# Low halves of streamed weights moved from GpSimd to VectorE in a single-core transformer kernel

## The reference

```
first_block:   h += 0.5 * swiglu(rmsnorm(h))                        # MLP1
               n  = rmsnorm(h);  z = n @ w_in                       # MIX1
               attn_o = sliding-window attention with rope and sinks(z)
               gla_o  = chunked gated linear attention(z), rmsnorm, * silu(gate)
               h += concat(attn_o, gla_o) @ w_out
               h += 0.5 * swiglu(rmsnorm(h))                        # MLP2
               h += sigmoid(rmsnorm(h) @ w_gate) * rmsnorm(p @ w_proj)   # PLE
second_block:  x += even_mixer(rmsnorm(x))      # EVEN: short conv and differential attention
               x += mem_attention(rmsnorm(x), rmsnorm(mem))         # CROSS0, 256 memory rows
               x += conv_ffn(rmsnorm(x))        # CONV0: up, conv of width 3, silu * value, down
               x += odd_mixer(rmsnorm(x))       # ODD: stick-breaking attention, 16 heads
               x += mem_attention(...)          # CROSS1
               x += conv_ffn(...)               # CONV1
```

## Time and profile before

| | |
|---|---|
| median of 3 runs | 2725.68 us |
| profiled execution | 2733.84 us |
| its span | 2731.7 us |
| busy: TensorE | 2626.6 us, 96% |
| busy: VectorE | 1462.8 us, 54% |
| busy: ScalarE | 908.0 us, 33% |
| busy: GpSimd | 473.1 us, 17% |
| mean granted TensorE clock | 0.985 |

### The profile page before, as it was taken

The page is one execution under the profiler, slowest core; times in us unless marked ns, Lnnn a source line. Parts: engine busy times, 40 slices in busy tenths (PEclk is TensorE's granted clock), DMA queues, the critical chain, the costliest instruction groups (busy, mean ns, idle before and its releaser), DMA issues.

```text
span 2731.7 us, 32426 instructions
## 1 busy us (share of the span) xinstructions
PE 2626.6 (96%) x12690; PEld 2147.6 (79%) x12690; DVE 1462.8 (54%) x1847; ACT 908.0 (33%) x1186; POOL 473.1 (17%) x352
## 2 busy tenths in 40 slices
PE   8999999889999988998999999999999999999999
PEld 6888877668888867876787888887886788888887
DVE  5444455665444467165543766565136554474745
ACT  4221243443211134433442423233136243332322
POOL 0000023122000013423453000003420354200000
PEclk9999999999999999999999999999999999999999
DMA  5222231013223222211332222323310133122222
GB/s 173 93 92 98 98 123 63 32 47 100 93 92 101 95 101 83 93 52 63 107 103 83 77 94 92 107 86 117 104 51 1 58 115 106 63 93 92 92 101 84
DMA packets 36597, 240.68 MB, mean 88 GB/s; under 512 B 3952, under 2 KB 6912, under 8 KB 8320
## 3 DMA queue, kind: packets, MB, share of 16 engines
q1 hardware_dynamic: 35008, 234.12, 24.9%
q10 hardware_dynamic: 1472, 4.94, 0.5%
HBM read 236.94 MB, written 2.10 MB: 88 GB/s over the span
## 4 chain that ended last, share of the span: by engine, by line
PE 87%; DVE 8%; ACT 2%; issue 1%; DMA 0%; DVEq 0%; SPq 0%; ACTq 0%
PE ps L494 23%; PE ps L495 23%; PE ps L496 23%; PE ps L1053 1%; PE ps L1006 1%; DVE op_lo L1602 1%; PE ps L978 1%; PE ps L512 1%; PE ps L511 1%; PE ps L510 1%; DVE sums L1616 1%; PE ps L522 1%; PE ps L606 1%; PE ps L607 1%; PE ps L608 1%
## 5 line engine op out<-in xcount | busy, mean ns | idle before, releaser
L494 PE MATMUL ps<-op_hi,w_hi 128*128 128x512 f32 x2160 | 856.7, 397 | 31.2 <-DVE op_lo L1602 21.3
L495 PE MATMUL ps<-op_lo,w_hi 128*128 128x512 f32 x2160 | 845.8, 392 | 0.0
L496 PE MATMUL ps<-op_hi,w_lo 128*128 128x512 f32 x2160 | 845.6, 392 | 0.0
L448 POOL TENSOR_TENSOR w_lo<-w_raw,w_hi 128x512 fp32r<-128x512 f32 x348 | 472.9, 1390 | 1892.5 <-ACT w_hi L1107 1892.3
L1107 ACT ACTIVATE w_hi<-w_raw 128x2048 fp32r<-128x2048 f32 x217 | 414.1, 1908 | 530.7 <-PE ps L496 404.8
L494 PEld LDWEIGHTS ps<-op_hi,w_hi 128*128 128x128 f32 x2160 | 408.9, 189 | 125.8 <-issue 20.1
L495 PEld LDWEIGHTS ps<-op_lo,w_hi 128*128 128x128 f32 x2160 | 408.9, 189 | 89.1 <-issue 4.9
L496 PEld LDWEIGHTS ps<-op_hi,w_lo 128*128 128x128 f32 x2160 | 408.6, 189 | 86.4
L1688 DVE TENSOR_TENSOR w_lo<-w_raw,w_hi 128x2048 fp32r<-128x2048 f32 x130 | 298.1, 2293 | 20.9 <-ACT w_hi L1107 8.1
L1653 DVE SCALAR_TENSOR_TENSOR x<-ps,x 128x512 f32<-128x512 f32 x134 | 92.6, 691 | 367.9 <-PE ps L496 357.4
L494 PE MATMUL ps<-h_hi,w_hi 128*128 128x512 f32 x692 | 273.4, 395 | 0.0
(11 more groups left out here) (286 smaller groups left out, 3070.2 us busy)
## 6 DMA issues: line engine op xcount, KB each, us to landing
w_raw<-in_wstream_dram SPq DMA_DIRECT2D x217, 1024.0 KB, 4.8
w_raw<-in_wstream_dram SPq DMA_DIRECT2D x8, 256.0 KB, 7.5
x<-in_x_dram SPq DMA_DIRECT2D x4, 512.0 KB, 7.1
cr_m<-in_mem_dram ACTq DMA_DIRECT2D x2, 1024.0 KB, 4.8
out_dram<-x SPq DMA_DIRECT2D x3, 512.0 KB, 2.6
ev_s<-in_alibi_dram ACTq DMA_DIRECT2D x1, 1024.0 KB, 4.8
m_c<-in_rope_dram ACTq DMA_DIRECT2D x1, 704.0 KB, 6.0
pl_p<-in_p_dram ACTq DMA_DIRECT2D x1, 512.0 KB, 3.6
```

Source lines behind the costliest of these rows:

```text
L448: ins = nc.gpsimd.tensor_tensor(w_lo[:, c % 4, at], w_raw[:, c % 2, at], w_hi[:, c % 4, at].bitcast(FP32), ALU.subtract)
L494: mm_(o, w_hi[:, c % 4, w], hi[:, k, 0:cols], start=(k == 0), stop=False)
L495: mm_(o, w_hi[:, c % 4, w], lo[:, k, 0:cols], start=False, stop=False)
L496: mm = mm_(o, w_lo[:, c % 4, w], hi[:, k, 0:cols], start=False, stop=(k == kt - 1))
```

## The change

GpSimd's program is removed. VectorE makes the low halves of all slabs with `low`, at hand-set points:

- `update_and_norm` calls `low(c + d + 3)` after each of the first three `onto_x` in every stage (in CROSS from the second on), not in MLPs alone.
- `mlp` begins with `low(at + 2)` where it waited for `w_ready`.
- In `attention` a `low` stands one iteration after each `between`.
- MIX1, EVEN and ODD have a `low` ahead of the first `use_rs_x` and after each `keep`; one of them stands right ahead of the sliding attention.
- In the gated linear attention `gl_scaled(l)` moves ahead of the `keep` at levels 3 and 6, and level 5 has a `low` behind it; another follows the output loop.
- PLE has a `low` before and after the last sums of squares and after each of three gates. CROSS has two ahead of the first `use_rs_x`, one ahead of its first `keep`, one after each `norm_queries`, one after `keep_values(0)`, and one an iteration after each of its entries in `CROSS_ENDS`.

```diff
-        @block.gpsimd
-        def _(pool):
-            def low(c):
-                n = SLAB // PIECES
-                for q in range(PIECES):
-                    at = slice(q * n, (q + 1) * n)
-                    ins = nc.gpsimd.tensor_tensor(w_lo[:, c % 4, at], w_raw[:, c % 2, at],
-                                                  w_hi[:, c % 4, at].bitcast(FP32), ALU.subtract)
-                ins.then_inc(w_ready, 1)
...
             def update_and_norm(...):
                 for d in range(DOWN - 1):
                     onto_x(c + d, d, 0, scale)
-                    if lows:
+                    if d >= first:
                         low(c + d + 3)
...
-                dve.wait_ge(w_ready, at + MLP_FIRST)
+                low(at + 2)
                 low(at + 3)
                 use_rs_x()
...
+                    if i - 1 in ends:
+                        low(c + ends[i - 1] + 3)
                     if i in ends:
                         between(ends[i])
...
             keep(c + 5, [m1_gk[:, 0, :], m1_gk[:, 1, :]])
+            low(c + 8)
             v.tensor_scalar(neg_sinks[:], gcol("sinks", 0, 8), -1.0, None, ALU.mult)
...
+                gl_scaled(l)
                 if l == 3:
                     keep(c + 8, [m1_gog[:, 0, :], m1_gog[:, 1, :]])
+                elif l == 5:
+                    low(c + 11)
                 elif l == 6:
                     keep(c + 9, [m1_gog[:, 2, :], m1_gog[:, 3, :]])
-                gl_scaled(l)
...
             keep_embedding(3, KT)
+            low(AT_PLE + 2)
             for k in range(KT):
                 add_squares(k)
+            low(AT_PLE + 3)
...
             for d in range(DOWN - 1):
                 gate(d)
+                low(AT_PLE + 4 + d)
...
+                low(at + 4)
                 for h in range(4):
                     keep(at + h, [cr_q[:, 2 * h, :], cr_q[:, 2 * h + 1, :]])
                     add_pair(h)
                     if h:
                         norm_queries(h - 1)
+                        low(at + h + 4)
...
             for d in range(4):
                 keep_rows(AT_ODD + 8 + d, od_v[:, :, d * 256:(d + 1) * 256])
+                low(AT_ODD + d + 11)
```

More of the change, by code:

```diff
@@ L56 @@
 PIECES = 4
-MLP_FIRST, MLP_END = 3, MLP_SLABS + 2
 TRI = 13 * P
@@ L1689, in low, with update_and_norm @@
                                 ALU.subtract).then_inc(w_ready, 1)
-            def update_and_norm(c, name, scale=1.0, also=None, early=False, lows=False):
+            def update_and_norm(c, name, scale=1.0, also=None, early=False, first=0):
                 for d in range(DOWN - 1):
                     onto_x(c + d, d, 0, scale)
-                    if lows:
+                    if d >= first:
                         low(c + d + 3)
@@ L1772, in mlp @@
                 n["taps"] += 2 * FT if conv else 0
-                update_and_norm(at + 24 + GROUPS[2], name, scale, also, early=True, lows=True)
+                update_and_norm(at + 24 + GROUPS[2], name, scale, also, early=True)
             def maxima(it, width, sinks=None):
@@ L1810, in probabilities, with attention @@
                     done(p_ready)
-            def attention(N, maxs, probs, outs, between, ends, beside={}):
+            def attention(N, maxs, probs, outs, c, between, ends, beside={}):
                 i0 = n["it"]
@@ L1850, in _ @@
             mlp(AT_MLP1, "mix")
+            c = AT_MIX1
+            low(c + 2)
             use_rs_x()
-            c = AT_MIX1
             cos, sin = m1_c[:, 0:SEQ], m1_c[:, SEQ:2 * SEQ]
@@ L1868, in _ @@
             keep(c, [m1_q[:, 0, :], m1_q[:, 1, :]])
+            low(c + 3)
             keep(c + 1, [m1_q[:, 2, :], m1_q[:, 3, :]])
+            low(c + 4)
             for t in range(2):
@@ L1872, in _ @@
             keep(c + 2, [m1_k[:], sums[0:16, :]])
+            low(c + 5)
             dve.wait_ge(aux["m1_c"], 16)
@@ L1885, in _ @@
                 rotated(m1_q[:, t, :])
+            low(c + 6)
             head_norm([m1_k[:]], [gcol("k")])
@@ L1888, in _ @@
             rotated(m1_k[:])
+            low(c + 7)
             dve.wait_ge(gate_ready, 1)
@@ L2021, in _ @@
                 operand(4 + h, tmp[:])
+            low(c + 12)
             update_and_norm(AT_MIX1 + MIX1_SLABS, "ffn2")
@@ L2071, in _ @@
                 gate(d)
+                low(AT_PLE + 4 + d)
             norm_x("mix0", lambda: gate(DOWN - 1))
+            low(AT_EVEN + 2)
             use_rs_x()
@@ L2120, in _ @@
                         head_norm([heads[t]], [gcol("eq" if t < 4 else "ek")])
+                low(c + d + 3)
             keep_rows(c + 5, ev_v[:, :, 256:512])
+            low(c + 8)
             dve.wait_ge(aux["lam"], 16)
@@ L2165, in cross @@
             def cross(at, layer):
+                low(at + 2)
+                low(at + 3)
                 use_rs_x()
@@ L2213, in cross @@
                 norm_queries(3)
+                low(at + 8)
                 norm_keys(0)
                 keep_values(0)
+                low(at + 9)
                 i0, N = n["it"], len(CROSS_ITEMS)
@@ L2245, in cross @@
                             keep_values(g)
+                    if i - 1 in CROSS_ENDS:
+                        low(at + CROSS_ENDS[i - 1] + 4)
                 n["it"] += N
-                update_and_norm(at + CROSS_SLABS, f"f{layer}")
+                update_and_norm(at + CROSS_SLABS, f"f{layer}", first=1)
             cross(AT_CROSS0, 0)
@@ L2251, in _ @@
             mlp(AT_CONV0, "mix1", True, 1.0)
+            low(AT_ODD + 2)
             use_rs_x()
@@ L2256, in _ @@
                 keep(AT_ODD + d, [od_q[:, 2 * d, :], od_q[:, 2 * d + 1, :]], scale=0.125)
+                low(AT_ODD + d + 3)
             for d in range(4):
                 keep(AT_ODD + 4 + d, [od_k[:, 2 * d, :], od_k[:, 2 * d + 1, :]])
+                low(AT_ODD + d + 7)
             for d in range(4):
                 keep_rows(AT_ODD + 8 + d, od_v[:, :, d * 256:(d + 1) * 256])
+                low(AT_ODD + d + 11)
             def softplus(t, kb):
```

4 lines of the change are left out of this document (2 added, 2 removed).

## The result

The kernel after takes 2699.65 us (median of 4 runs, 2698.73 to 2703.06), against 2726.43 us of the kernel before (median of 4 runs beside it, 2724.35 to 2728.99). The ratio is 0.9904, with a 95% interval of 0.9886 to 0.9921, which is small but clear of 1: faster by 26.8 us, where 26.6 us were forecast. The profiled execution after took 2699.93 us, its span is 2697.7 us.

The account below looks back on a forecast made before the run. TensorE was taken to bound the kernel, so time could change only where it stops or runs at a lower clock. Gains of -29.9 and costs of +3.3 make -26.6 us: 2699 us, range 2687 to 2717 us.

Parts of the forecast that it names:

- Rival 4: VectorE's stretched operations are not GpSimd's doing, so the added lows cost: slower, 2736 us; chance 0.04.
- The three starts: Entries to MIX1, ODD and PLE: stretched operations shorten, TensorE's stops and clock loss shrink or go: -4.9, -4.9, -8.7 us.
- rival 1: TensorE's stops shorten but the clock doesn't come back, with less from levels and PLE to EVEN: 2709 us; chance 0.22.
- Levels, -3.3: Gated linear attention: gl_scaled ahead of the keep shortens TensorE's stops of 3.03 and 1.61 us: -3.3 us.
- Sliding attention, +2.2: A low right ahead of the sliding attention's first maxima delays the probabilities TensorE waits for: +2.2 us, between 0 and 2.3.
- PLE's gates, -2.7: PLE to EVEN: relieved gate operations give about 9.5 us, three lows take 6.9, EVEN's op_lo comes earlier: -2.7 us.
- EVEN: Stretched probabilities ahead of a stop of 1.74 us, -1.4 us; stretched cast and subtraction at the output, -1.3 us.
- ODD's output: The same stretched cast and subtraction as at EVEN's output, with no low ahead: -1.8 us.
- rival 2: More gain: EVEN's entry and two output stops go wholly warm, PLE to EVEN gives -6: 2689 us; chance 0.11.
- CROSS1: A cost of +0.1 us in this stage, beside +0.5 us for the low ahead of CROSS's first keep.
- Rival 5: VectorE's lows block on w_hi, exposed in the attentions; sign: wait over 15 us; 2731 us at 14 exposed; chance 0.04.
- Rival 3: Stage starts: freed time turns into waits for ScalarE's op_hi; with costs at upper ends (+3.7), 2724 us; chance 0.07.

Follow-up runs that it names:

- changed_again: The kernel after the change, unaltered, run again as the base of a group of runs: 2698.44 us, ratio 0.9900 to the kernel before.
- pool_writes: The kernel after, with GpSimd given eight memsets per slab in MIX1, PLE and EVEN that read nothing and that nobody waits for: 2699.32 us, ratio 0.9897.
- pool_reads: The kernel after, with GpSimd given eight subtractions per slab in MIX1, PLE and EVEN that read SBUF and that nobody waits for: 2723.54 us, ratio 0.9985.
- pool_whole: The kernel before, with GpSimd's four pieces of each slab joined to one instruction of 128x2048: 2754.58 us, ratio 1.0100.
- entries_only: The kernel before, with only the third slab of MIX1, PLE and ODD moved from GpSimd to VectorE: 2711.08 us, ratio 0.9936.
- keep_ahead: The kernel after, with the two keep calls at levels 3 and 6 put ahead of gl_scaled again: 2699.41 us.
- three_later: The kernel after, with three lows (sliding attention, level 5, PLE's third gate) moved to where VectorE was idle: 2694.75 us and, measured again, 2696.67 us.

## Why the prediction was right

The sum was 26.6 us and the medians give 26.8; in two groups of the experiments the same TensorE and VectorE programs gained 28.3 us (changed_again) and 29.7 us (pool_writes). The mechanism is the forecast's. That the sum fits to 0.2 us is luck: terms that were off cancel, as the table shows.

- *Contention as the cause: shown.* Recreated without any dependency it takes 24 of 30 us back, if in part in other places than they were gained (pool_reads), and without GpSimd's reads nothing is lost (pool_writes). Rival 4 is out. The size that I took from the rows, 0.8 to 1.0 us an operation, was right for the pieces of 128x512; the reason behind it was incomplete. I set the rows against a full lock; pool_whole shows that there is one, and the ends of pieces and operations show that the rows are its result with alternating turns, 1.67 to 1.70 us for each pair of a piece and an operation. The four operations of rows 6 also add up to 6.56 us, not to 6.44.
- *The three starts.* -4.9, -4.9 and -8.7 forecast; 4.8, 4.7 and 9.7 in the profiles; entries_only, which does these alone, gave 18 of 18.5 us. PLE's stops came out at 3.67 and 0.55 us (3.6 and under 1 forecast; the second is 1.76 us in changed_again). The clock terms came with them: MIX1 begins at a granted clock of 1.00, so that rival 1 is out where stops went. The size of that term, 2.1 us, doesn't follow from its figures, though, which give 4.4 - 13 x 0.23 = 1.4; of the 4.8 us of the matched traces 3.0 are there when the stop ends, which leaves 1.7 for it.
- *Levels, -3.3: the term's reason failed.* I held that the wait of a `keep` ahead of `gl_scaled` fed TensorE's stops and that the reordering ends them. keep_ahead shows that it gives nothing: ScalarE's `gl_a` is as late. With the old order and without GpSimd it gained 3.6 us from the end of the sliding attention to behind the levels, the two profiles of the change 2.5 and 3.6. So what the levels gained is the missing contention (2.9 us by the earlier trace rows, of which I had given 2.3 to the low). The 1.5 us of the line "first levels" are the moved `keep` alone: keep_ahead has nothing there, and has caught up 7 us later. TensorE's waits for L741's kind sum to 7.8 us, as forecast (some 8), but 3.4 of them are ScalarE's now.
- *Sliding attention, +2.2: too large, by how much is open.* The low delays the start by 2.15 us, as the row said. The profiles with it lose 0.8 to 2.3 us in the stage, those with the low moved 0 to 1.4. The granted clock changes between executions within this stage, and by as much as the term.
- *PLE's gates, -2.7:* 1.8. The stretches there add up to 10.8 us in the trace, not to 9.5, so that the term's own reasoning gives -3.9. It left out that the low behind the third gate would hold up the `op_lo` ahead, a new stop of 1.09 us, which three_later removes. With *EVEN* (-1.4 and -1.3: 2.2 and 0.9) the sum was right to 0.5 us, but for EVEN's attention not by its reason alone: the stop there fell by 0.65 us only (1.74 to 1.09), and the rest is the clock, 0.71 behind it before and 1.00 after. *CROSS0* (+0.5) gave 0.2 back: at +0.2 us TensorE's wait for the pair sums hardly grew (5.8 to 6.0 us). *ODD* (+0.5) came.
- *ODD's output: a clock term was left out.* 4.4 us for a forecast of 1.8. The stop fell from 4.02 to 2.21 us, which is my 1.8; the rest is the clock. Behind the stop of about 4 us it was 0.50 in the kernel before and 0.68 in entries_only, behind the stop of 2.21 us it was 1.00 in eight of nine profiles and 0.69 in pool_reads. So this is the change's doing in most executions, and a part of what rival 2 had.
- *CROSS1* shows 3.6 us for a forecast of -0.1, behind a stop that the change doesn't alter. The same stretch is at full clock in entries_only too, which has the same program there as the kernel before and is 3.1 us shorter in CROSS1 than it. So I take these 3.1 us as that one execution's and not the change's, which fits that it was 8.16 us above its median, and that of after 0.3 above its own. That is argued from two profiles, not shown. The other 0.5 us are the change's: in CROSS1 it cost nothing.
- *Rival 5's mark was crossed, without harm.* VectorE waited for `w_hi` for 17.2 us in 12 lows (8.1 in 3 before), over the 15 that I had set as the sign of it. TensorE's timelines show none of the stops that it would have caused: no matmul waits for one of the 87 lows, and the weight loads wait for lows 1.0 us in four waits. *Rival 3* is out: the waits for `op_hi` are still 17.6 us. (Its +3.7 for the costs at their upper ends is more than the stated ends give, 1.9.)
- *"Early everywhere" was not quite so.* At EVEN's output in the kernel before, GpSimd's slab was done at 1270.78 us, 3.5 us into TensorE's stop of 4.19. The stop went by VectorE's `op_lo`, which was done at 1271.33, so that the sum doesn't suffer.

## What to carry to other kernels

An engine that is idle 83% of the time and hardly ever waited for can still set the end: look at how long the same instruction takes beside it and alone, and where that lies on a chain that TensorE waits for. Three of 87 moved subtractions were worth some 60% of the gain (18 of 30 us in one group), those whose helper ran in the last microseconds before a stage began; to find them, go by TensorE's stops and not by busy shares. If work must stay on GpSimd beside VectorE, cut it into short instructions, since each holds the other engine for its whole length: whole slabs made this kernel 1.0% slower than quarters.

## What the runs showed of the hardware

- A VectorE operation with two SBUF operands that starts behind a GpSimd instruction reading SBUF waits for its end: 4.87 us for one of 0.75 (GpSimd's 4.88 us long, in pool_whole), 1.67 us beside four pieces that took 6.67, 1.11 us beside eight pieces that took 8.04. It ends 0.55 us behind the piece. A cast is stretched too (1.54 us for 0.43). A GpSimd memset doesn't stretch it (0.75 us).
- GpSimd pays as well: its piece of 128x512 takes from 1255 to 1814 ns, with a mean of 1390; in one piece a slab takes 4.6 us, and 401.6 us for all 87, not 473.1.
- The granted clock is not a function of the stop alone. Behind the same stop of 2.68 us in CROSS1 it was 0.50 over 5 us in one profiled execution and full in ten of eleven of other kernels, worth some 3 us. This moves a single execution of this kernel by more than most terms of such a sum.
